# Paged sample keys: TensorE transposes replaced by VectorE 32x32 block transposes, and host matmul pieces redistributed

## Chip, cores and metric

The kernel runs on one core of one Trainium2 chip. The metric is the device time of one launch in microseconds (us), the median of several executions. Engines are named as in the profile: PE is TensorE's matmul side and PEld its weight loads, DVE is VectorE, ACT is ScalarE, POOL is GpSimd, SP is SyncE. SPq and POOLq are the queues on which SP and POOL issue DMAs.

## What is computed

Two layers of a hybrid decoder for a prompt of 1024 tokens and 8 samples of 4 new tokens each; layer 0 mixes a short convolution with differential attention. The change is in one part of layer 0: the samples' attention over a paged cache of 2048 past keys and values (16 pages of 128 rows for each sample, 4 heads of 128 numbers, all float32).

```python
past_k = cache_k[j, page_table].reshape(nb, -1, DA_HEADS, 2 * DA_DIM)
past_v = cache_v[j, page_table].reshape(nb, -1, DA_HEADS, 2 * DA_DIM)
...
s = jnp.einsum('bqhcd,bkhcd->bhcqk', q, k).astype(jnp.float32) * (DA_DIM ** -0.5)
s = jnp.where(mask, s, -jnp.inf)
p = jax.nn.softmax(s, axis=-1)
w = p[:, :, 0] - lam * p[:, :, 1]
return jnp.einsum('bhqk,bkhe->bqhe', w.astype(v.dtype), v)
```

The same layer's input projection `u @ w_in` has further columns (gates and values of the convolution) that don't depend on the samples' attention; their matmuls are spread between its steps.

## The kernel before

Every engine's program is written out by hand, in order, with semaphores. The samples' stage is `pe_samples`, `act_samples`, `dve_samples` and `sp_samples`; each is a generator of steps. `woven` runs such a generator and, after each step, as many **host pieces** as a table says: a host piece is half of a unit of the input projection (12 matmuls 128x352, fp16, line L372), and 27 units make 54 pieces. The units come in threes: three units of `gate_c` (drained from PSUM by ACT, L1513), three of the convolution's input (drained by DVE, L1574), three of `y_b` (drained by DVE, L1593, after the three convolution taps L1538 to L1545). All units of this stage use one PSUM bank, so a unit starts only when the one before it has been drained. The same weave holds for all four engines: in DVE's program a drain stands at the place at which PE's program has the second piece of that unit.

The stage works in two rounds of 4 samples. A round has a **key phase** (32 steps `q` of 2 pages), a **softmax gap**, a **value phase** (32 steps of 2 pages) and a short tail.

- Key step before: PE waits for two pages in the ring, transposes 2x4 blocks 128x128 into PSUM banks 4 and 5 (L1943), ACT and DVE copy one bank each to `kt` in SBUF (L2012, L2072), and `scores(q-1)` multiplies the turned keys of the step before with the queries in 4 matmuls (L1931), one for each head; the four write 32 partitions each of one bank. Scores of a round fill PSUM banks 0 to 3.
- Softmax gap: own keys (L1954), maxima on DVE (L2067, L2079), exponentials on ACT (L2018), and matmuls that mix the two halves (L1960 to L1967).
- Value step: 8 matmuls against 2 value pages (L1982).

Pages are 256 KB each and go into a ring of 16 (`ring`, in `hT`). `load_page` issues page `f` when `page_used` says that page `f - 16` is free; SP issues the pairs with even `f // 2`, POOL the others. `page_used` rises when PE has transposed a key page or has used a value page. SP's queue also holds the loads of projection weights (L287), each waiting until a split (L345 on DVE) has freed its buffer.

`ROUND_FILL` is the table of host pieces: before, none in the 32 key steps, 8 in the softmax gap, 15 in the value steps (one after every second), 3 in the tail.

`pool_queries` builds the block-diagonal queries `q_blk` on POOL after the key and value rows of head 3 have been stored.

Of the kernel before, what the change touches and what calls it, by code (L numbers as in the profile page):

```python
# [78 lines left out]
def build(nc, x_p, x_s, cache_k, cache_v, state_conv, state_C, state_n, state_m, page_table, norms, w_in0,  # L79
# [3 lines left out]
    with ctx:  # L83
# [1359 lines left out]
        sm_max, sm_neg = small[:, 80:85], small[:, 85:86]  # L1443
# [8 lines left out]
        wt_own = arena[0:TS, 23, 0:64]  # L1452
        comb = arena[:, 23, 64:128]
        kt = [arena[:, 24 + i, 0:SEQ].rearrange("p (h n) -> p h n", h=HEADS) for i in range(2)]
# [66 lines left out]
        def dve_proj0(dve, chain, v0, v1_):  # L1521
# [24 lines left out]
            for n in range(VISITS[v0].units[0], VISITS[v1_].units[-1] + 1):  # L1546
                v, g, x = UNITS[n].visit, UNITS[n].g, ps[:, UNITS[n].bank, :]
                h, m = (v - CXB) // 3 if v >= CXB else v // 3, v % 3
                if v >= CXB and m == 2 and g == 0:
                    if h == 0:  # L1550
                        dve.wait_ge(q_ready, 1)
# [315 lines left out]

        ROUND_FILL = ((0,) * 32 + (2, 2, 2, 2) + (1, 0) * 15 + (0, 0) + (1, 1, 1))
# [40 lines left out]
        def pe_samples(pe):  # L1909
# [1192 lines left out]
```

## Time and profile before

| | us |
|---|---|
| median of 3 runs | 2692.53 |
| lowest, highest | 2690.15, 2693.31 |
| the profiled execution's own time | 2693.54 |
| its span, first to last instruction | 2691.9 |
| PE busy, of the span | 2623.9 (97%) |
| DVE, ACT, POOL busy | 1242.1, 1026.6, 452.3 |

The profiled execution is 1.0 us above the median, and 1.6 us of its time lie outside the span. The samples' stage takes from about 315 to 574 us of the span. Busy shares are averages over stages with different limits, so the rows further down look at this stage in stretches. An "us" beside a group of several instructions is the time from the start of the first to the end of the last; the modelled duration of a single matmul is longer than the distance between two.

### The profile page before, as it was taken

To read this page: it belongs to the slowest core of one execution; us is meant where nothing else is said; L and a number is where in the kernel's file an instruction comes from. 1 tells how busy PE (TensorE), PEld (TensorE's weight loads), DVE (VectorE), ACT (ScalarE), POOL (GpSimd) and SP (SyncE) were. 2 spreads that over 40 slices of the span, in tenths; PEclk is the share of its full clock that TensorE was granted. 3 is DMA by queue.
4 is the path that set the end of the run, shared out by engine and by line. 5 is a ranking of instruction groups with operands and counts; after the bars stand their busy time and mean duration, and the time that the engine had idled before them with its cause. 6 is when DMAs were issued, how large, how long until landed. Compare 5 with 4: busy or idle time off the path is not lost.

```text
span 2691.9 us, 49459 instructions
## 1 busy us (share of the span) xinstructions
PE 2623.9 (97%) x20217; PEld 1876.5 (70%) x20217; DVE 1242.1 (46%) x2042; ACT 1026.6 (38%) x1896; POOL 452.3 (17%) x529
## 2 busy tenths in 40 slices
PE   8999899999999999999999999999999999999998
PEld 5666566656688668886566766667657886788765
DVE  5555532326744214444754434344577441154454
ACT  4455322225444214433443333324365441244333
POOL 4001023222022002311101010110101220123121
PEclk9999999999999999999999999999999999999999
DMA  7211369761211312124434242322411122011442
GB/s 250 63 40 50 98 218 346 242 230 54 75 64 32 81 53 63 48 91 146 122 88 88 40 115 50 96 67 84 151 54 67 64 60 60 32 64 48 134 129 97
DMA packets 257659, 266.14 MB, mean 99 GB/s; under 512 B 10668, under 2 KB 217810, under 8 KB 256796
## 3 DMA queue, kind: packets, MB, share of 16 engines
q1 hardware_dynamic: 231772, 166.10, 22.0%
q0 software_dynamic: 25088, 94.79, 10.0%
q8 instruction: 162, 2.65, 0.4%
q10 hardware_dynamic: 576, 2.10, 0.2%
q14 instruction: 61, 0.50, 0.1%
HBM read 227.45 MB, written 35.50 MB: 98 GB/s over the span
## 4 chain that ended last, share of the span: by engine, by line
PE 90%; DVE 5%; ACT 2%; issue 1%; DMA 0%; POOL 0%; SPq 0%; DVEq 0%; ACTq 0%; POOLq 0%
PE ps L372 49%; PE ps L1130 25%; PE ps L1943 2%; PE ps L1931 1%; PE ps L1629 1%; PE ps L1982 1%; PE ps L1708 1%; PE ps L2477 1%; PE ps L2457 1%; PE ps L2491 1%; PE ps L2513 1%; DVE arena L883 1%; PE ps L1694 1%; PE ps L2500 1%; DVE hT L887 1%
## 5 line engine op out<-in xcount | busy, mean ns | idle before, releaser
L372 PE MATMUL ps<-u,w_split 128*128 128x352 f16 (+1 forms) x4752 | 752.3, 315 | 9.8 <-DVE u L737 5.9
L372 PEld LDWEIGHTS ps<-u,w_split 128*128 128x128 f16 (+1 forms) x4752 | 462.5, 98 | 260.3 <-issue 20.8
L372 PE MATMUL ps<-arena,w_split 128*128 128x352 f16 x3663 | 560.6, 313 | 3.7 <-DVE w_split L345 1.5
L372 PEld LDWEIGHTS ps<-arena,w_split 128*128 128x128 f16 x3663 | 357.6, 98 | 200.8 <-issue 9.5
L1130 PE MATMUL ps<-hT,w_split 128*128 128x264 f16 x3456 | 400.6, 276 | 3.2 <-ACT arena L1170 3.2
L1130 PEld LDWEIGHTS ps<-hT,w_split 128*128 128x128 f16 x3456 | 337.8, 98 | 54.8 <-DVE w_split L345 2.1
L345 DVE SCALAR_TENSOR_TENSOR w_split<-w_raw,w_split 128x1024 f16<-128x1024 f32 (+2 forms) x133 | 184.5, 1388 | 296.4 <-ACT w_split L329 295.8
L1130 PE MATMUL ps<-u,w_split 128*128 128x264 f16 x2592 | 303.4, 276 | 0.0
L1130 PEld LDWEIGHTS ps<-u,w_split 128*128 128x128 f16 x2592 | 253.6, 98 | 38.3
L329 ACT ACTIVATE w_split<-w_raw 128x1024 f16<-128x1024 f32 (+2 forms) x133 | 155.5, 1171 | 135.9 <-PE ps L372 97.3
L343 DVE SCALAR_TENSOR_TENSOR w_split<-arena,w_split 128x512 f16<-128x512 f32 x126 | 85.9, 723 | 103.9 <-ACT w_split L323 103.9
L1260 POOL TENSOR_TENSOR arena<-arena 128x512 f32<-128x512 f32 x18 | 22.8, 1265 | 527.2 <-DVE w_split L343 527.2
L343 DVE SCALAR_TENSOR_TENSOR w_split<-w_raw,w_split 128x512 f16<-128x512 f32 x126 | 80.8, 686 | 62.4 <-ACT w_split L323 62.4
L372 PE MATMUL ps<-arena 128*128 128x352 f16 x657 | 102.6, 316 | 0.0
L2327 ACT ACTIVATE arena<-ps 128x352 f32<-128x352 f32 x66 | 30.5, 464 | 179.7 <-PE ps L372 179.7
L817 POOL TENSOR_TENSOR arena<-arena 128x352 f32<-128x352 f32 x53 | 71.3, 1345 | 160.5 <-ACT arena L805 160.3
L1203 DVE TENSOR_TENSOR arena<-ps,arena 128x528 f32<-128x528 f32 x36 | 25.5, 707 | 153.1 <-ACT arena L1170 153.1
L1300 ACT ACTIVATE arena<-ps 128x352 f32<-128x352 f32 x48 | 22.3, 465 | 191.3 <-PE ps L372 191.3
L372 PEld LDWEIGHTS ps<-arena 128*128 128x128 f16 x657 | 64.5, 99 | 37.0 <-issue 3.1
L1216 DVE TENSOR_TENSOR arena<-arena 128x1056 f16<-128x1056 f32 (+1 forms) x60 | 58.3, 972 | 50.4 <-ACT arena L1153 41.4
L372 PE MATMUL ps<-u,arena 128*128 128x352 f16 x504 | 77.5, 313 | 3.2 <-ACT arena L1298 2.7
L323 ACT ACTIVATE w_split<-arena 128x512 f16<-128x512 f32 x126 | 71.7, 620 | 13.7 <-PE ps L1130 10.9
(405 smaller groups left out, 2989.4 us busy)
## 6 DMA issues: line engine op xcount, KB each, us to landing
w_raw<-in_w_down SPq DMA_DIRECT2D x58, 704.0 KB, 4.7
w_raw<-in_w_in SPq DMA_DIRECT2D x56, 512.0 KB, 7.9
arena<-in_w_gu SPq DMA_DIRECT2D x18, 1024.0 KB, 5.3
w_raw<-in_w_gu SPq DMA_DIRECT2D x18, 1024.0 KB, 5.2
hT<-in_cache_k SPq DMA_DIRECT2D x64, 256.0 KB, 4.4
hT<-in_cache_k POOLq DMA_DIRECT2D x64, 256.0 KB, 4.6
hT<-in_cache_v SPq DMA_DIRECT2D x64, 256.0 KB, 5.0
hT<-in_cache_v POOLq DMA_DIRECT2D x64, 256.0 KB, 5.5
```

Of the source, the lines that this page charges most:

```text
L323: act.activation(split_of(v, 0).rearrange("p (k n) -> p k n", k=kt), raw_of(v), ACT.Copy, scale=WS).then_inc(w_hi, 1)
L329: act.activation(split_of(v, 0)[:, 0:kt * n], raw_of(v), ACT.Copy, scale=WS).then_inc(w_hi, 1)
L343: dve.scalar_tensor_tensor(lo, raw_of(v), WS, hi, ALU.mult, ALU.subtract).then_inc(w_ready, 1)
L345: dve.scalar_tensor_tensor(split_of(v, 1)[:, 0:kt * n], raw_of(v), WS, split_of(v, 0)[:, 0:kt * n], ALU.mult, ALU.subtract).then_inc(w_rea ...
L372: ins = pe.matmul(ps[0:m, bank, 0:GW], split_of(v, wp)[:, k * w + col * P:k * w + col * P + m], x[:, xp, k0 + k, cols(g)], start=(k == 0 a ...
L817: pool.tensor_tensor(sum_y, sum_y, sq_y[k % 2], ALU.add).then_inc(y_added, 1)
L883: ins = dve.scalar_tensor_tensor(h_tmp[:, k % 2, :], ybuf[:, k, cols(g)], gains[:, col:col + 1], rs[0], ALU.mult, ALU.mult)
L887: dve.tensor_tensor(h, h, h_tmp, ALU.add).then_inc(h_ready, 1)
L1130: ins = pe.matmul(ps[:, bank + s_, 0:HW], split_of(v, wp)[:, k * P:(k + 1) * P], x, start=(name in ("M1", "M2", "M5") and k == 0 and q == ...
L1216: dve.tensor_tensor(hi_lo[:, 1], x, hi_lo[:, 0], ALU.subtract).then_inc(hid_ready, 1)
L1943: ins = pe.transpose(ps[:, 4 + e, h * P:(h + 1) * P], ring[:, f % RING, h * P:(h + 1) * P], ident[:, :])
L2327: act.activation((q_of[h % 2], k1, v1, o1)[m // 2][:, m % 2, cols(g)], ps[:, UNITS[n].bank, 0:GW], ACT.Sigmoid if m >= 6 else ACT.Copy, sc ...
```

## The change

Key pages are no longer transposed by PE. DVE transposes 32x32 blocks of two ring pages at once (one instruction, 128x1024) into one row of a buffer `turned[j]`; four of them fill a buffer of 8 pages, and there are two buffers. A block transpose leaves block (i, c) in place, so the keys of partition group i and column group c lie turned within each 32x32 block. PE then scores 8 pages at once, in 64 matmuls with 32 partitions and 32 columns of weights: row group `i` uses keys 32i to 32i+31, four shifts `s_` cover the four blocks of a head, head `h` picks the column group, and row group `i` writes PSUM bank `i`. For this the queries are needed in four rotations by 32 partitions; `pool_queries` makes one and copies three by DMA, and it moves ahead of the stores of head 3. The key phases of ACT's program become empty. The maxima of a round become one reduction 128x2048. Half of the host pieces of the value steps go into the key steps: 8 in the key steps (after every fourth), 8 in the gap, 7 in the value steps, 3 in the tail. `wt_own` and `comb` move to another buffer.

```diff
-        q_blk = arena[:, 19, 0:SEQ].rearrange("p (h b n) -> p h b n", h=HEADS, b=NB)
+        Q_ROWS = (10, 12, 13, 14)
+        q_turned = [arena[:, row, 0:SEQ].rearrange("p (h b n) -> p h b n", h=HEADS, b=NB) for row in Q_ROWS]
+        q_blk = q_turned[0]
-        kt = [arena[:, 24 + i, 0:SEQ].rearrange("p (h n) -> p h n", h=HEADS) for i in range(2)]
+        turned = [rows(19 + 4 * i, 4)[:, :, 0:SEQ] for i in range(2)]
...
-            pool.wait_ge(v_ev, 3 * HEADS - 1)
+            pool.wait_ge(s_done, 16 * (HEADS - 1))
...
+            pool.wait_ge(q_copied, 2 * NB)
+            for s_ in range(1, 4):
+                cut = P - 32 * s_
+                pool.dma_start(arena[0:cut, Q_ROWS[s_], 0:SEQ], arena[32 * s_:P, Q_ROWS[0], 0:SEQ]).then_inc(q_ready, 16)
+                pool.dma_start(arena[cut:P, Q_ROWS[s_], 0:SEQ], arena[0:32 * s_, Q_ROWS[0], 0:SEQ]).then_inc(q_ready, 16)
...
-        ROUND_FILL = ((0,) * 32 + (2, 2, 2, 2) + (1, 0) * 15 + (0, 0) + (1, 1, 1))
+        ROUND_FILL = ((0, 0, 0, 1) * 8 + (2, 2, 2, 2) + (0, 1, 0, 0) * 7 + (0,) * 4 + (1, 1, 1))
...
-                def scores(q):
-
-                    n, b, j = 32 * r_ + q, 4 * r_ + q // 8, q % 8
-                    pe.wait_ge(kp_ev[0], n + 1)
-                    pe.wait_ge(kp_ev[1], n + 1)
+                def scores(n):
+
+                    b, j = 4 * r_ + n // 2, n % 2
+                    pe.wait_ge(page_used, 128 * r_ + 8 * n + 8)
                     pe.wait_ge(exps, 5 * r_)
-                    for h in range(HEADS):
-                        ins = pe.matmul(ps[32 * h:32 * h + 32, j // 2, 256 * (j % 2):256 * (j % 2) + 256],
-                                        q_blk[:, h, b, :], kt[n % 2][:, h, :], start=(b % 4 == 0 and j % 2 == 0),
-                                        stop=(b % 4 == 3), skip_group_check=True)
-                    ins.then_inc(kp_used, 1)
+                    pages = turned[j].rearrange("p a (e c) -> p a e c", e=2)
+                    for s_ in range(4):
+                        for h in range(HEADS):
+                            for i in range(4):
+                                part_, e0 = slice(32 * i, 32 * i + 32), P * h + 32 * ((i + s_) % 4)
+                                ins = pe.matmul(ps[32 * h:32 * h + 32, i, 256 * j:256 * j + 256],
+                                                q_turned[s_][part_, h, b, :], pages[part_, :, :, e0:e0 + 32],
+                                                start=(b % 4 == 0 and j == 0 and s_ == 0),
+                                                stop=(b % 4 == 3 and s_ == 3), skip_group_check=True)
+                    ins.then_inc(scored, 1)
+                for q in range(32):
+                    if q % 4 == 3:
+                        scores(q // 4)
+                    yield
...
-                    dve.wait_ge(page_used, 128 * r_ + 2 * q + 2)
-                    dve.wait_ge(kp_used, max(n - 1, 0))
-                    dve.tensor_copy(kt[n % 2][:, :, P:2 * P],
-                                    ps[:, 5, :].rearrange("p (h e) -> p h e", h=HEADS)).then_inc(kp_ev[1], 1)
+                    f = 128 * r_ + 2 * q
+                    dve.wait_ge(page_loaded[f % RING // 2], 32 * (f // RING + 1))
+                    if q >= 8:
+                        dve.wait_ge(scored, 8 * r_ + q // 4 - 1)
+                    dve.transpose(turned[q // 4 % 2][:, q % 4, :],
+                                  ring[:, f % RING:f % RING + 2, :].rearrange("p r c -> p (r c)")).then_inc(page_used, 2)
...
-                chain.link(dve.tensor_reduce(sm_max[:, 4:5], ps[:, 4, 0:TS], AX.X, ALU.max))
+                chain.mark(dve.tensor_reduce(sm_max[:, 0:1], flat(0, 4 * 512), AX.X, ALU.max))
+                chain.link(dve.tensor_reduce(sm_max[:, 1:2], ps[:, 4, 0:TS], AX.X, ALU.max))
```

PE, start of the first key phase, in the program before. L1943 are transposes, L1931 scores, and no host piece (L372) stands between:

```order
L1643 MATMUL ps<-ident,arena 128x128 x4
L1943 MATMUL ps<-ident,hT 128x128 x16
L1931 MATMUL ps<-arena 32x256 x4
L1943 MATMUL ps<-ident,hT 128x128 x8
L1931 MATMUL ps<-arena 32x256 x4
```

And now, the end of that key phase (the pair of L1938 and L372 stands there 8 times, and the last is shown):

```order
L1938 MATMUL ps<-arena 32x256 x64
L372 MATMUL ps<-u,w_split 128x352 x12
L1949 MATMUL ps<-ident,smask 128x32
L1953 MATMUL ps<-arena 32x32 x16
L372 MATMUL ps<-u,w_split 128x352 x48
```

The transposes are gone, 8 blocks of 64 small matmuls stand where 32 groups of 4 stood, and each is followed by one host piece.

DVE, end of the first round's tail and the second key phase, in the program before:

```order
L2108 SCALAR_TENSOR_TENSOR arena<-ps,gains,arena 128x16 x4
L1574 SCALAR_TENSOR_TENSOR arena<-ps,arena 128x352
L2072 COPY arena<-ps 128x4x128 x28
L2067 TENSOR_REDUCE small<-ps 128x1
L2072 COPY arena<-ps 128x4x128 x2
```

And now, from the second block's end to the fourth drain. L1575 and L1594 are drains of host units, L1539, L1542 and L1545 convolution taps:

```order
L2065 STREAM_TRANSPOSE arena<-hT 128x1024 x8
L1575 SCALAR_TENSOR_TENSOR arena<-ps,arena 128x320
L1579 SCALAR_TENSOR_TENSOR arena<-ps,arena 128x8x4
L2065 STREAM_TRANSPOSE arena<-hT 128x1024 x4
L1554 COPY conv_new<-arena 128x2
L1555 COPY conv_new<-arena 128x16
L1539 TENSOR_SCALAR arena<-arena,gains 128x1024
L1540 TENSOR_SCALAR arena<-arena,gains 128x32
L2065 STREAM_TRANSPOSE arena<-hT 128x1024 x4
L345 SCALAR_TENSOR_TENSOR w_split<-w_raw,w_split 128x1024
L1542 SCALAR_TENSOR_TENSOR arena<-arena,gains 128x1024
L1543 SCALAR_TENSOR_TENSOR arena<-arena,gains 128x32
```

Drains and taps, which stood behind the key phases, now stand between transposes, after 8, 16, 24 and 32 of them in this round, and after 24 and 32 in the first.

## Rows read from the trace of the kernel before

**Rows 1.** The page, part 4: engines' shares of the chain that ended last.
```profile
PE 90%; DVE 5%; ACT 2%; issue 1%; DMA 0%; POOL 0%; SPq 0%; DVEq 0%; ACTq 0%; POOLq 0%
```
**Rows 2.** Windows: us, busy (instructions) of PE, PEld, DVE, ACT, POOL, PE clock, DMA share, GB/s.
```profile
315.25:369.29 54.04, 53.78 (x547) 34.60 (x547) 24.61 (x36) 19.12 (x32) 17.27 (x32) 0.97 0.92 309
369.29:391.55 22.26, 20.20 (x133) 13.83 (x130) 3.83 (x11) 6.70 (x15) 0.00 (x0) 0.92 0.16 55
391.55:437.79 46.24, 46.08 (x726) 28.64 (x726) 11.80 (x21) 5.84 (x10) 15.72 (x29) 1.00 0.97 337
437.79:445.55 7.76, 6.75 (x47) 4.47 (x46) 3.10 (x12) 3.48 (x13) 1.61 (x3) 1.00 1.03 353
445.55:497.76 52.21, 51.61 (x542) 32.79 (x540) 24.66 (x37) 20.36 (x33) 17.20 (x32) 1.00 0.93 315
497.76:517.76 20.00, 18.63 (x133) 12.95 (x130) 9.48 (x23) 5.59 (x14) 0.00 (x1) 1.00 0.18 56
517.76:564.00 46.24, 46.08 (x726) 28.63 (x726) 11.27 (x20) 5.34 (x9) 13.02 (x25) 1.00 0.88 309
```
**Rows 3.** Timeline, two key steps: start, us, engine, line, what, count [idle before, releaser].
```profile
339.81 0.40 PE L1931 MATMUL ps<-arena 128*32 128x256 f32 x4
...
341.16 0.16 PEld L1931 LDWEIGHTS ps<-arena 128*32 128x32 f32 x8 [0.17 <-issue]
341.16 0.64 PE L1931 MATMUL ps<-arena 128*32 128x256 f32 x8
341.27 0.69 DVE L2072 COPY arena<-ps 128x512 f32<-128x512 f32 x1 [0.90 <-PE ps L1943]
...
341.73 1.09 PE L1943 MATMUL ps<-ident,hT 128*128 128x128 f32 x8
...
342.75 0.64 PE L1931 MATMUL ps<-arena 128*32 128x256 f32 x8
```
**Rows 4.** Timeline and one line's durations: matmuls on two row groups in layer 1.
```profile
1543.59 1.14 PE L2513 MATMUL ps<-arena,hT 32*128 32x258 f32 x8
1544.66 0.62 PE L372 MATMUL ps<-u,w_split 128*128 128x352 f16 x3
...
L2513 PE MATMUL ps<-arena,hT x128: 376/376/480, 1543.6 to 1927.2; 32*128 32x258 f32 x128
```
**Rows 5.** Timeline of DVE: single instructions of 1024 elements, one behind the other.
```profile
397.98 0.75 DVE L1538 TENSOR_SCALAR arena<-arena,gains 128x1024 f32<-128x1024 f32 x1
...
400.06 1.28 DVE L1541 SCALAR_TENSOR_TENSOR arena<-arena,gains 128x1024 f32<-128x1024 f32 x1
401.25 0.24 DVE L1542 SCALAR_TENSOR_TENSOR arena<-arena,gains 128x32 f32<-128x32 f32 x1
```
**Rows 6.** Timeline: value steps with one host piece, and the drain behind it.
```profile
395.20 1.96 PE L372 MATMUL ps<-u,w_split 128*128 128x352 f16 x12
397.10 1.06 PE L1982 MATMUL ps<-hT,arena 128*4 128x128 f32 x32
...
397.20 0.49 DVE L1574 SCALAR_TENSOR_TENSOR arena<-ps,arena 128x320 f32<-128x320 f32 x1 [5.02 <-PE ps L372]
```
**Rows 7.** Timeline: before the first key phase, and the own keys at its end.
```profile
314.15 0.75 DVE L1812 SCALAR_TENSOR_TENSOR arena<-ps,gains,arena 128x512 f16<-128x512 f32 x1 [0.40 <-ACT arena L1731]
315.25 3.67 PE L1943 MATMUL ps<-ident,hT 128*128 128x128 f32 x16 [1.86 <-issue]
...
368.46 0.90 PE L1954 MATMUL ps<-arena 128*32 128x32 f32 x32
```
**Rows 8.** Windows around the start of the first key phase (columns as in rows 2).
```profile
312.00:315.50 3.50, 1.64 (x13) 1.00 (x12) 2.50 (x3) 1.15 (x2) 0.00 (x0) 1.00 0.08 21
315.50:318.90 3.40, 3.40 (x20) 2.54 (x22) 0.69 (x1) 1.20 (x2) 0.23 (x1) 0.50 0.84 225
318.90:322.30 3.40, 3.40 (x40) 2.14 (x40) 1.53 (x3) 1.19 (x2) 0.91 (x2) 1.00 0.60 170
```
**Rows 9.** A window inside the first value phase, and DMA issues of that phase.
```profile
406.00:422.00 16.00, 16.00 (x262) 9.97 (x260) 3.24 (x5) 2.40 (x4) 5.39 (x10) 1.00 1.05 384
...
hT<-in_cache_v SPq DMA_DIRECT2D x24, 256.0 KB, 6.1
```
**Rows 10.** Timeline: two reductions 128x1024 on DVE, and the query copies on POOL.
```profile
290.59 2.35 DVE L1781 TENSOR_REDUCE small<-ps 128x1 f32<-128x1024 f32 x2
...
248.83 4.89 POOL L1863 COPY arena<-arena 64x16 f32<-64x16 f32 x16
```

More of the change, by code:

```diff
@@ L1442, in build @@
         zx, zy, zz = (small[:, 56 + 8 * i:64 + 8 * i] for i in range(3))
-        sm_max, sm_neg = small[:, 80:85], small[:, 85:86]
+        sm_max, sm_neg = small[:, 80:82], small[:, 85:86]
         sm_sum, sm_scale = small[:, 86:91], small[:, 91:92]
@@ L1550, in dve_proj0 @@
                     if h == 0:
[L1551 removed]
+                        dve.wait_ge(q_copied, 2 * NB)
                     chain.sync()
@@ L1855, in pool_queries @@
         def pool_queries(pool, chain):
-            pool.wait_ge(v_ev, 3 * HEADS - 1)
+            pool.wait_ge(s_done, 16 * (HEADS - 1))
             drained(pool, last_unit(3 * HEADS - 3))
-            chain.link(pool.memset(arena[:, 19, 0:SEQ], 0.0))
+            chain.link(pool.memset(arena[:, Q_ROWS[0], 0:SEQ], 0.0))
             for b in range(NB):
@@ L1935, in pe_samples @@
                 if r_:
                     pe.wait_ge(os_lo, 1)
-                for q in range(32):
-                    for e in range(2):
-                        f = 128 * r_ + 2 * q + e
-                        page_ready(f)
-                        pe.wait_ge(kp_ev[e], 32 * r_ + q)
-                        for h in range(HEADS):
-                            ins = pe.transpose(ps[:, 4 + e, h * P:(h + 1) * P], ring[:, f % RING, h * P:(h + 1) * P],
-                                               ident[:, :])
-                        ins.then_inc(page_used, 1)
-                    if q:
-                        scores(q - 1)
-                    yield
@@ L1949, in pe_samples @@
-                scores(31)
                 pe.matmul(ps[:, 4, 0:TS], smask[:, r_, :], ident[0:TS, 0:TS], start=True, stop=False,
@@ L2008, in act_samples @@
                 for q in range(32):
-                    n = 32 * r_ + q
-                    act.wait_ge(page_used, 128 * r_ + 2 * q + 1)
-                    act.wait_ge(kp_used, max(n - 1, 0))
-                    act.activation(kt[n % 2][:, :, 0:P], ps[:, 4, :].rearrange("p (h e) -> p h e", h=HEADS),
-                                   ACT.Copy).then_inc(kp_ev[0], 1)
                     yield
@@ L2016, in act_samples @@
                 act.wait_ge(max_ready, r_ + 1)
-                for j in range(4):
-                    act.activation(probs[:, 512 * j:512 * j + 512], ps[:, j, :], ACT.Exp, bias=sm_neg,
-                                   accum_out=sm_sum[:, j:j + 1]).then_inc(exps, 1)
+                for i in range(4):
+                    act.activation(probs[:, 0:2 * SEQ].rearrange("p (f i t) -> p i f t", i=4, t=32)[:, i],
+                                   ps[:, i, :].rearrange("p (f t) -> p f t", t=32), ACT.Exp, bias=sm_neg,
+                                   accum_out=sm_sum[:, i:i + 1]).then_inc(exps, 1)
                 act.activation(probs[:, 2 * SEQ:2 * SEQ + TS], ps[:, 4, 0:TS], ACT.Exp, bias=sm_neg,
@@ L2849, in _ @@
             for h in range(HEADS):
+                if h == HEADS - 1:
+                    pool_queries(pool, chain)
                 for ev, src, dst, n in ((v_ev, v_nat, v_p, 2), (k_ev, k_nat, k_p, 2)):
@@ L2853, in _ @@
                                    src.rearrange("p (c a e) -> p c a e", c=8, a=1)).then_inc(kv_stored, 16)
-            pool_queries(pool, chain)
             pool.wait_ge(v_ev, 3 * HEADS)
```

23 lines of the change are left out of this document (7 added, 16 removed).

## Prediction

> **What bounds the kernel now.** The page's chain comes first: nine tenths of it are PE [rows 1], so what counts is PE's time and what PE waits for. Then the windows that cut the samples' stage at its phases [rows 2]. In all four key and value phases PE is busy for all but 0.2 to 0.6 us, while ACT and DVE work less than half of a key phase; only the two softmax gaps (22.26 and 20.00 us) and the tail of round 0 (7.76) show PE waiting, 1 to 2 us each. A second column matters as much: DMAs run at 309 to 337 GB/s in the phases, and inside the value phase at 384 [rows 9]. PE bounds the stage, and a DMA limit lies close behind. Last come two key steps in the timeline [rows 3]: from one group of scores to the next 1.59 us (341.16 to 342.75), of which 0.57 are scores and 1.02 the 8 transposes.
>
> **Scores and transposes on PE.** What goes is 32 steps of 1.59 us in each round. What comes is 8 blocks of 64 matmuls. A float32 matmul is two records (4 matmuls of a step show x8), so a block has 128 records. Do small tiles overlap? In a step four records start within 0.40 us, in which each of them runs nearly its whole length, and all 8 take 0.64 [rows 3]: four column groups run at once, the second four 0.24 behind the first. L2513 does the same with two row groups: 8 records, 376 ns each, in 1.14 us, and the next group starts 1.07 after the first [rows 4]. So I take all 16 tiles of 4 row and 4 column groups to run at once, which no row shows. Then a block is 8 passes: four passes take 1.07, two take 0.57, so each further one is 0.25, and 8 are 1.07 + 4 x 0.25 = 2.1 us. Bounds: 16 passes if only 8 tiles overlap (0.57 + 14 x 0.25 = 4.1), 32 passes if only 4 do (8.1). I take 2.1, since neither the row nor the column groups cost anything for each other where they are seen. One host piece takes 1.9 us up to the next work, and the drain on DVE starts 2.0 after the piece's start and takes 0.5 [rows 6]. PE needs 2.1 + 1.9 = 4.0 us for a block.
>
> The Trainium skill, "TensorE: Matmul & The Clock Gate", Part 3, gives 10.6 times the serial speed for 16 tiles of 32x32; serial, 128 records at 0.24 us would be 31 us, and by that figure a block is 2.9 us, an estimate, 0.8 more than mine, which would add about 5 us to the whole over four drains and two tails. The same page (Part 1) says that starts of small matmuls never come closer than about 25 ns. The row with four records in 0.40 us [rows 3] speaks against it: the fourth would start 75 ns behind the first and, at 376 ns of its own [rows 4], end at 0.45. By the rule a block would be 3.2 + 0.3 = 3.5 us and the whole some 10 us above my sum, at 2690, no change; its chance is part of the second one below.
>
> **Transposes on DVE.** No row has this instruction. The nearest is a float32 instruction of 1024 elements from SBUF to SBUF: L1541, whose follower starts 1.19 us later. L1538 takes 0.75 for the same size [rows 5], and a PSUM copy 0.69 for 512 [rows 3], so 1.38 for 1024. I take 1.2, since a transpose reads and writes 1024 numbers in each partition as L1541 does, and keep 0.75 and 1.38 as ends. Four make a block: 4.8 us. So DVE, not PE (4.0), sets the pace of the key phases. The ring doesn't: 16 pages are there at the start, and at 384 GB/s 8 pages take 5.5 us, so that DVE in six blocks (28.8 us) uses what DMA can bring (16 pages, and 32 more in 22 us after the first frees).
>
> **The new wait.** A drain that stands in DVE's program behind a block of transposes waits for the host unit's second half, which PE starts only behind the scores of that same block. What is queued behind it on DVE are the next transposes, and PE waits for these in turn. So each drain costs DVE 2.1 + 2.0 + 0.5 = 4.6 us, and PE then idles 0.5 + 4.8. Round 0 has one inside (block 5) and one at the end; round 1 has three inside (blocks 1, 3, 5) and one at the end. Convolution taps moved into round 1: the first (L1539 and its small neighbours, 1.1 us by their starts) is on DVE's path, the other two with L345, 4.1 us, lie in the wait at block 3.
>
> **The clock.** Where PE had been idle 1.86 us just before 315.25 [rows 7], its clock was granted at 0.50 (1.2 GHz) from 315.5 to 318.9, and at 1.00 (2.4 GHz) next to it [rows 8]: 16 transposes took 3.67 us, 1.6 more than two groups of 8. I charge 1.7 us of PE for each idle of about 5 us. PE has 0.8 of slack in a block, so 0.9 reaches the next drain: once in round 0, three times in round 1.
>
> **Key phases.** Transposes can start when L1812 ends, at 314.90 [rows 7], where PE's start at 315.25. Round 0: 38.4 (8 x 4.8) + 4.6 (drain) + 0.9 (clock) + tail of 2.1 + 1.9 + own keys 0.8 (368.46 to 369.29) = 48.7, so it ends at 363.6 where it ended at 369.29: **-5.7**. Round 1: 38.4 + 3 x 4.6 + 0.2 (second small drain) + 1.1 (tap) + 2.7 (clock) + 4.8 (tail) = 61.0 against 52.21: **+8.8**. Eight host pieces (15 us) are done in each of them, which is why it is the value phase that gains.
>
> **Value phases.** PE's work falls from 15 to 7 pieces: 32 steps x 0.5 (two are one group of 1.06) [rows 6] + 7 x 1.9 = 29.3 us, where 15 pieces made 44.5 of the 46.24. But now DMA ends last: of 64 pages 16 are in the ring, the other 48 are 12.6 MB and take 32.8 us at 384 GB/s [rows 9]. With 3.0 until the first lands (half of the 6.1 us of a landing under full load), 1.4 for a weight tile of 0.5 MB among them and 0.5 for the last step it is 37.7 against 46.24: **-8.5 each, -17.0**.
>
> **Gaps, tail, POOL.** The drains rotate: the first gap gets the pieces that the second had, and the second nearly those of the first, so 22.26 + 20.00 stay together. The single maximum over 2048 columns takes 2.35 (two of 1024) [rows 10] where one over 512 stood behind the last scores; PE has two host pieces (3.8 us) there, which hide most of it, and I charge 0.5 a round: **+1.0** (bounds 0 and 3.4). On ACT 32 copies a round vanish, which waited for PE anyway: 0. POOL's copies (4.89 us) [rows 10] and six new DMAs stand ahead of the stores of head 3 and long before the first key phase: 0; if the stores came late, DVE's first transposes would wait for them. SP's weight loads wait for splits on DVE behind transposes; the pages queued behind them have 9 us until they are needed: 0.
>
> **Sum.** -5.7 + 8.8 - 17.0 + 1.0 = -12.9. The profiled execution took 2693.54, so 2680.6; it is 1.0 above the median of before, so I say **2680 us**.
>
> **Rivals.** (1) *Tiles overlap less.* Eight at a time: block 4.1, PE 6.0 a block, each drain 6.6. Round 0 becomes 4.8 + 48 + 5.3 + 0.8 = 59 (before 54.4 from 314.90), round 1 four pairs of 4.8 + 6.0 + 4.1 + 2.5 and 0.3 = 70: +4.6 + 18 - 17 + 1 gives 2700. Four at a time: 8.1, so 10.0 a block and 86 in either round: +31 + 34 - 17 + 1 gives 2742. For it: no row has more than four at once, and four row groups would write four banks of the same partitions together. Against it: rows 3 and 4. It decides from a block of 3.9 us upwards, where round 1 has eaten the value phases' gain. This is the case that ends slower. (2) *Slower transposes.* At 1.38 us, +11.5, so 2691: no change. At twice my value 77 us more, 2757; nothing in the rows speaks for that. (3) *DMA doesn't hold 384 GB/s.* At the value phases' mean of 337, 48 pages take 37.3 and a phase 42.4, so only -3.8 each: 2689. For it: the DMA share is 0.97 already in that phase; against it: the 16 us at 384. (4) *DVE is faster.* At 0.75 a block of transposes is 3.0 and PE's 4.0 sets the pace: 14 us less in round 0, 4 in round 1, with the value phases 2658.
>
> **Chances.** My forecast with its own spread (2672 to 2687) 0.45; rivals 2 (mild) and 3, and the forecast's upper edge, 2687 to 2698, 0.19; eight tiles or a mixture, 2698 to 2708, 0.13; four tiles or very slow transposes 0.12; rival 4 and anything below 2672, 0.11. Range 2662 to 2708: it leaves out 0.12 above and some 0.05 below. A measurement tells 0.2% (5.4 us): faster 0.56, same 0.18, slower 0.26.
>
> **What will show it.** Transposes of 1.2 us, one behind the other but for one long wait on PE in the first key phase and three in the second, each ended by L372. Groups of 128 records of 32x32 in about 2.1 us. Stretches of granted clock 0.50 behind these waits. Value phases of about 38 us in which PE waits for DMA of value pages, with 380 GB/s. Key phases of about 49 and 61 us. I am wrong if a scoring block takes over 3 us, if DVE doesn't wait for L372, or if PE still ends the value phases without waiting for pages.

## Result and profile after

| | before | after |
|---|---|---|
| median, us | 2691.69 (4 runs) | 2703.06 (4 runs) |
| lowest, highest | 2690.15, 2693.31 | 2700.26, 2708.56 |
| profiled execution, its span | 2693.54, 2691.9 | 2700.58, 2699.0 |

The change makes the kernel slower: ratio 1.005, 95% interval 1.0038 to 1.0062, so 10 to 17 us. I had said 2680, 13 us faster. The profiled execution of after is 7.0 us above that of before, at the low end of its runs.

The page, part 4 (the chain that ended last), answers [rows 1]. PE holds 74% of it where it held 90%:

```profile
PE 74%; DVE 4%; ACT 2%; issue 1%; DMA 1%; SPq 1%; POOL 0%; DVEq 0%; ACTq 0%
```

Windows of after, answering [rows 2] (us, busy of PE, PEld, DVE, ACT, POOL, PE clock, DMA share, GB/s): key phase, gap, value phase, tail, and the second round's key phase, gap and value phase.

```profile
313.50:372.52 59.02, 43.59 (x1154) 26.25 (x1155) 39.20 (x37) 3.16 (x4) 17.28 (x32) 0.88 0.87 305
372.52:395.66 23.14, 20.31 (x133) 13.56 (x131) 11.67 (x24) 5.59 (x14) 0.00 (x0) 0.93 0.08 24
395.66:436.91 41.25, 33.34 (x629) 21.04 (x629) 3.53 (x5) 3.78 (x6) 15.87 (x30) 0.92 0.97 350
436.91:445.76 8.85, 7.67 (x44) 4.19 (x40) 3.05 (x12) 3.44 (x12) 1.33 (x3) 0.81 1.05 374
445.76:512.98 67.22, 45.66 (x1154) 27.90 (x1155) 44.26 (x49) 3.05 (x5) 17.37 (x32) 0.82 0.78 263
512.98:533.58 20.60, 18.54 (x133) 12.90 (x131) 6.97 (x13) 7.61 (x18) 0.00 (x0) 1.00 0.11 31
533.58:575.45 41.87, 32.75 (x630) 21.18 (x629) 7.78 (x15) 1.55 (x2) 13.12 (x24) 0.96 0.92 326
```

In both key phases PE, busy for all of them before, now idles 15 and 22 us, at a mean clock of 0.88 and 0.82. Against before, with the first key phase counted from 314.90 as in the prediction: key phases +4.6 and +15.0, value phases -5.0 and -4.4, gaps +0.9 and +0.6, tail +1.1, and the stage begins 1.4 earlier. That is +11.4 at the end of the second value phase (575.45 for 564.00). Behind the stage 4.3 us of it come back; there before's clock is lower in places (0.97 for 1.00 from 575 to 700 us), which the change doesn't touch.

Timeline of DVE in after, from the sixth block of the first key phase on (start, us, engine, line, what, count, idle before and its releaser):

```profile
341.33 4.62 DVE L2065 STREAM_TRANSPOSE arena<-hT 128x1024 f32<-128x1024 f32 x4 [1.70 <-PE ps L1938]
345.88 1.18 DVE L345 SCALAR_TENSOR_TENSOR w_split<-w_raw,w_split 128x1024 f16<-128x1024 f32 x1
...
354.68 0.53 DVE L1575 SCALAR_TENSOR_TENSOR arena<-ps,arena 128x352 f32<-128x352 f32 x1 [7.47 <-PE ps L372]
355.12 9.12 DVE L2065 STREAM_TRANSPOSE arena<-hT 128x1024 f32<-128x1024 f32 x8
371.46 0.53 DVE L1575 SCALAR_TENSOR_TENSOR arena<-ps,arena 128x352 f32<-128x352 f32 x1 [7.23 <-PE ps L372]
```

Transposes are as forecast, 4.62 us a block. From their end at 345.95 to the next at 355.12 there are 9.2 us, where I had 5.5 with the clock. PE at the same time:

```profile
336.35 0.69 PE L1938 MATMUL ps<-arena 32*32 32x256 f32 x26
338.88 2.31 PE L1938 MATMUL ps<-arena 32*32 32x256 f32 x102 [1.83 <-issue]
...
348.54 2.76 PE L1938 MATMUL ps<-arena 32*32 32x256 f32 x128
351.23 0.32 PE L372 MATMUL ps<-u,w_split 128*128 128x352 f16 x1
352.82 1.81 PE L372 MATMUL ps<-u,w_split 128*128 128x352 f16 x11 [1.27 <-issue]
359.79 4.53 PE L1938 MATMUL ps<-arena 32*32 32x256 f32 x128 [5.15 <-DVE arena L2065]
```

A scoring block takes 2.76 us at full clock and 4.53 behind this idle of 5 us (4.08 to 4.52 behind those of the second key phase). And there is something that I hadn't thought of: inside a block, or a host piece, PE stands for 0.4 to 1.8 us with nothing to wait for ("issue"; such an idle is called a stall below). A window of that idle and block, and the next, with the clock in the last column but two:

```profile
358.80:365.60 6.80, 5.81 (x133) 3.42 (x134) 5.44 (x5) 0.00 (x0) 2.69 (x5) 0.50 0.89 312
365.60:369.40 3.80, 3.80 (x136) 2.40 (x134) 0.00 (x0) 0.00 (x0) 1.08 (x2) 1.00 1.04 395
```

The second key phase on DVE has the three inner waits and the one at the end:

```profile
462.87 0.49 DVE L1575 SCALAR_TENSOR_TENSOR arena<-ps,arena 128x320 f32<-128x320 f32 x1 [7.99 <-PE ps L372]
...
478.94 0.53 DVE L1594 SCALAR_TENSOR_TENSOR arena<-ps,arena 128x352 f32<-128x352 f32 x1 [1.17 <-PE ps L372]
...
495.63 0.52 DVE L1594 SCALAR_TENSOR_TENSOR arena<-ps,arena 128x352 f32<-128x352 f32 x1 [6.73 <-PE ps L372]
...
511.92 0.52 DVE L1594 SCALAR_TENSOR_TENSOR arena<-ps,arena 128x352 f32<-128x352 f32 x1 [6.33 <-PE ps L372]
```

### The profile page after: what moved, and what is told of

Its sections match the earlier page's. It is cut to its first block, busy times and chain, and to the rows that moved or that the text cites. A ratio compares the mean times of both kernels' runs of the same rounds, so it can differ in the third digit from the quotient of the medians.

```text
span 2699.0 us, 51203 instructions
## 1 busy us (share of the span) xinstructions
PE 2576.1 (95%) x21241; PEld 1844.4 (68%) x21241; DVE 1268.8 (47%) x2036; ACT 988.3 (37%) x1832; POOL 455.9 (17%) x535
## 4 chain that ended last, share of the span: by engine, by line
PE 74%; DVE 4%; ACT 2%; issue 1%; DMA 1%; SPq 1%; POOL 0%; DVEq 0%; ACTq 0%
PE ps L372 41%; PE ps L1130 25%; PE ps L2468 1%; PE ps L2448 1%; PE ps L2482 1%; PE ps L2504 1%; DVE arena L883 1%; PE ps L2491 1%; DVE hT L887 1%; DVE arena L897 1%; DMA hT<-in_cache_v 1%; PE ps L2532 1%; PE ps L1938 1%; PE ps L2483 1%; DVE arena L2065 0%
## 5 line engine op out<-in xcount | busy, mean ns | idle before, releaser
L372 PE MATMUL ps<-u,w_split 128*128 128x352 f16 (+1 forms) x4752 | 754.2, 315 | 12.9 <-DVE u L737 5.9
L372 PEld LDWEIGHTS ps<-u,w_split 128*128 128x128 f16 (+1 forms) x4752 | 462.6, 99 | 268.6 <-issue 27.2
L372 PE MATMUL ps<-arena,w_split 128*128 128x352 f16 x3663 | 559.0, 313 | 3.7 <-DVE w_split L345 1.5
L372 PEld LDWEIGHTS ps<-arena,w_split 128*128 128x128 f16 x3663 | 357.0, 98 | 199.7 <-issue 9.4
L345 DVE SCALAR_TENSOR_TENSOR w_split<-w_raw,w_split 128x1024 f16<-128x1024 f32 (+2 forms) x133 | 184.4, 1387 | 285.1 <-ACT w_split L329 284.6
L372 PE MATMUL ps<-arena 128*128 128x352 f16 x657 | 101.0, 313 | 0.0
L2318 ACT ACTIVATE arena<-ps 128x352 f32<-128x352 f32 x66 | 30.5, 464 | 179.7 <-PE ps L372 179.7
L1938 PE MATMUL ps<-arena 32*32 32x256 f32 x2048 | 56.5, 466 | 37.6 <-DVE arena L2065 32.4
L372 PEld LDWEIGHTS ps<-arena 128*128 128x128 f16 x657 | 64.0, 98 | 36.2 <-issue 3.1
L372 PE MATMUL ps<-u,arena 128*128 128x352 f16 x504 | 79.0, 316 | 3.2 <-ACT arena L1298 2.7
```

Of the source, the lines that this page charges most:

```text
L345: dve.scalar_tensor_tensor(split_of(v, 1)[:, 0:kt * n], raw_of(v), WS, split_of(v, 0)[:, 0:kt * n], ALU.mult, ALU.subtract).then_inc(w_rea ...
L372: ins = pe.matmul(ps[0:m, bank, 0:GW], split_of(v, wp)[:, k * w + col * P:k * w + col * P + m], x[:, xp, k0 + k, cols(g)], start=(k == 0 a ...
L1938: ins = pe.matmul(ps[32 * h:32 * h + 32, i, 256 * j:256 * j + 256], q_turned[s_][part_, h, b, :], pages[part_, :, :, e0:e0 + 32], start=(b ...
L2318: act.activation((q_of[h % 2], k1, v1, o1)[m // 2][:, m % 2, cols(g)], ps[:, UNITS[n].bank, 0:GW], ACT.Sigmoid if m >= 6 else ACT.Copy, sc ...
```

## Experiments

The theory behind them: the places of host pieces in the key phases, with drains that wait, cost what the transposes and the value phases give. The rival: the scoring blocks themselves, by their length, the half clock and the issue stalls, are too slow wherever the pieces stand. Kernel before had a median of 2689.2 to 2689.7 us beside them (2691.69 beside after); each ratio is against the runs beside it. "Key phases" are from the first transpose to the end of the own keys, in us. Line numbers move by one to three between kernels. The three "unloaded" kernels have one run each, so their totals can't be set against a scatter of 6 to 16 us in the others; what is read from them are the lengths of phases in their profiles.

| kernel | median | ratio to before (95%) | key phases |
|---|---|---|---|
| after | 2703.06 | 1.0038 to 1.0062 | 59.0, 67.2 |
| fill_back | 2688.03 | 0.9978 to 1.0000 | 49.9, 48.8 |
| before_new_fill | 2709.09 | 1.0056 to 1.0089 | |
| drains_later | 2696.59 | 1.0018 to 1.0038 | 59.0, 59.7 |
| splits_aligned | 2686.79 | 0.9977 to 0.9996 | 54.8, 55.2 |
| kept_warm | 2701.01 | 1.0026 to 1.0057 | 58.2, 64.4 |
| half_scores | 2682.46 | 0.9959 to 0.9986 | 50.3, 57.5 |
| pieces_first | 2683.05 | 0.9961 to 0.9982 | 56.2, 54.8 |
| six_in_keys | 2687.99 | 0.9979 to 1.0000 | 50.9, 54.4 |
| four_in_keys | 2690.25 | 0.9993 to 1.0010 | 51.3, 57.3 |
| keys_unloaded | 2692.02, one run | | 52.4, 67.2 |
| back_unloaded | 2667.52, one run | | 41.1, 40.1 |
| values_unloaded | 2687.82, one run | | 60.3, 68.2 |

**fill_back: only the table of pieces undone.**

```diff
-ROUND_FILL = ((0, 0, 0, 1) * 8 + (2, 2, 2, 2) + (0, 1, 0, 0) * 7 + (0,) * 4 + (1, 1, 1))
+ROUND_FILL = ((0,) * 32 + (2, 2, 2, 2) + (1, 0) * 15 + (0, 0) + (1, 1, 1))
```

> The changed kernel with the old table of host pieces: none in the key phases, 15 in each value phase. Theory (the host pieces and their drains in the key phases are what costs): DVE sets the pace, 8 blocks of 4.62 us, then one scoring block of 2.7 and the own keys, 0.8: 40.5 us a key phase, 44 with some issue stalls; value phases back at 46.2. Against the changed kernel's 59.0 + 67.2 + 41.25 + 41.9 that is 174 to 181 for 209, so 2672 to 2680, below the kernel before. Rival (the scoring blocks themselves are too slow, wherever the pieces stand): PE, idle for 2 us in each block, stays at the half clock, a block takes 4.5 us and issue stalls of 1 us come on top, so PE sets 5.5 a block: 48 us a key phase, 2689, no better than before.

2688.0: the rival's number. Going back to the old table wins 15 us (2703 to 2688), the whole loss; the transposes on DVE by themselves gain between 0 and 0.2%. PE in its first key phase:

```profile
332.48 4.51 PE L1938 MATMUL ps<-arena 32*32 32x256 f32 x127 [0.60 <-issue]
338.79 4.07 PE L1938 MATMUL ps<-arena 32*32 32x256 f32 x128 [1.80 <-issue]
344.83 4.07 PE L1938 MATMUL ps<-arena 32*32 32x256 f32 x127 [1.97 <-issue]
```

Each of these rows begins in the middle of a block and runs into the next. From one to the next it takes 4.7 to 6.0 us where DVE needs 4.6. Stalls and half clock come together here, but a stall doesn't always lower the clock: in after, five stalls of up to 1.83 us left it at 1.00 from 322 to 358 us.

The rival's account fits the first key phase only. In the second, PE waits for DVE (15.5 us in seven places), and DVE for key pages. DVE in the first key phase:

```profile
328.20 5.84 DVE L2065 STREAM_TRANSPOSE arena<-hT 128x1024 f32<-128x1024 f32 x5 [1.82 <-issue]
334.99 2.37 DVE L2065 STREAM_TRANSPOSE arena<-hT 128x1024 f32<-128x1024 f32 x2 [0.94 <-DMA hT<-in_cache_k]
```

The first of these waits is put down to issue, but the trace has the landing of the page that it reads 0.08 us before it starts, and so it is, within 0.12 us, for every transpose that waited for "issue" in these kernels. Late pages cost DVE 3.7 and 4.1 us in fill_back's key phases, and 1.7 and 0 in after's.

**before_new_fill: the table alone, in the kernel before** (the same two lines the other way round).

> The kernel before with the new table of host pieces: 8 in each key phase, 7 in each value phase. Theory (the value phases become DMA-bound, so that moving pieces out of them doesn't pay even): PE bounds the key phases, +8 x 1.9 = +15.2 each; the value phases end by DMA at about 41.5 for 46.24, -4.7 each; +21 in sum, 2713. Rival (moving is neutral, since PE has the same work): 2692. If the waits of drains behind key steps cost extra here too, more than 2713.

2709.1, 20 above before. The first key phase goes from 54.0 to 66.7 us (315.96 to 382.67), +12.7 for 8 pieces (in a profiled execution 5 us above the median), the first value phase from 46.24 to 44.0 (402.67 to 446.65), since DMA ends it. So moving pieces out of value phases is a loss by itself while PE bounds the key phases.

**drains_later: the places on DVE one block later.**

```diff
+ROUND_LATE = ((0,) * 4 + (0, 0, 0, 1) * 6 + (0, 0, 0, 2) + (2, 2, 2, 2) + (0, 1, 0, 0) * 7 + (0,) * 4 + (1, 1, 1))
-woven(dve_samples(dve, chain), dve_proj0(dve, chain, CXB + 3, WO0 - 1), SAMPLE_FILL)
+woven(dve_samples(dve, chain), dve_proj0(dve, chain, CXB + 3, WO0 - 1), (1, 1, 0) + ROUND_LATE * 2)
```

> The changed kernel with the pieces' places on DVE one block (4 steps) later than on PE in the key phases; the last two fall together at the end of the phase. A drain then finds its unit done. Theory (the waits of drains cost 4 x about 8 us): PE sets the pace with 2.75 + 1.9 = 4.65 a block; first key phase 4.6 + 37.2 + 0.8 + issue stalls of 3 to 5 = 46 to 48 for 59.0, the second 48 to 52 for 67.2 (its taps, 4.1 us of DVE, now lie open): -26 or so, 2675 to 2681. Rival (issue stalls and the half clock set PE's time, and the waits only hide them): first phase unchanged at 57 to 59, second about 58: 2690 to 2695.

Neither: 2696.6, and the first key phase is no shorter. The inner drain waits 1.68 for 7.47 us, but a new wait has come, on DVE and SP's queue (timeline):

```profile
351.29 1.18 DVE L345 SCALAR_TENSOR_TENSOR w_split<-w_raw,w_split 128x1024 f16<-128x1024 f32 x1
352.55 0.39 SPq L287 DMA_DIRECT2D w_raw<-in_w_in  x1
353.70 4.30 SPq L1883 DMA_DIRECT2D hT<-in_cache_k  x4
...
360.67 4.62 DVE L2066 STREAM_TRANSPOSE arena<-hT 128x1024 f32<-128x1024 f32 x4 [5.85 <-DMA hT<-in_cache_k]
```

The split (L345) is later too; the weight load (L287) waits for it on SP's queue, and four key pages stand behind that load.

**splits_aligned: SP's places later as well.**

```diff
-woven(sp_samples(sp), sp_proj0(sp, CXB + 3, WO0 - 1), SAMPLE_FILL)
+woven(sp_samples(sp), sp_proj0(sp, CXB + 3, WO0 - 1), (1, 1, 0) + ROUND_LATE * 2)
```

> As drains_later, and SP's places for the weight loads are one block later too, so that a weight load doesn't wait on SP's queue, with key pages behind it, for a split that now comes one block later on DVE. Theory (the 5.85 and 5.14 us for which DVE waited for key pages in drains_later come from that): both waits go, -9 to -11, so 2686 to 2689 beside drains_later's 2696.6. Rival (the DMAs were full and the pages late anyway): no change, 2695 to 2697.

Held: both waits for pages are gone, -9.8 us. With the inner drains no longer waited for, the kernel is 16 us below after; DVE's remaining long wait of the first phase, 6.76, is the drain behind its last block. One of its 10 runs took 10509 us; I have no cause for it. Without it the median is 2686.22.

**kept_warm: 28 transposes of the identity ahead of the blocks that follow a long wait.**

```diff
+                    if n == 6 or (r_ and n % 2 == 0):
+                        for _ in range(28):
+                            pe.transpose(ps[:, 5, 0:P], ident[:, :], ident[:, :])
```

> The changed kernel with 28 transposes of the identity into an unused PSUM bank (about 3.7 us) ahead of the scoring blocks that follow a long idle: block 6 of the first key phase, blocks 0, 2, 4 and 6 of the second. They fill the idle of 5.2 us and add no wait. Theory (the half clock behind an idle makes a block 4.5 for 2.75 us and passes this on to the next drain): 1.8 to 3 us less at each of 3 to 4 drains, -7, so 2696 for 2703. Rival (the clock's loss lies in slack and costs nothing): 2703. If the added instructions stall as well, up to 2 us more.

2701.0: not to be told from after. Three of the five blocks ran in 2.75 behind idles of 2.1 to 2.2 us, and two in 4.1 at lower clock behind 2.1 and 2.3:

```profile
458.13 3.22 PE L1933 MATMUL ps<-ident 128*128 128x128 f32 x28
463.69 4.08 PE L1941 MATMUL ps<-arena 32*32 32x256 f32 x128 [2.34 <-DVE arena L2068]
```

The key phases are 0.8 and 2.8 us shorter in the profile. So the clock, though plain in the rows, is worth some 4 us there by this one profile, where the medians differ by 2, less than their scatter. The remedy was only half tried: it kept the full clock three times of five.

**half_scores: two of four shifts.** Half of the scoring is left out.

```diff
-                    for s_ in range(4):
+                    for s_ in range(2):
-                                                stop=(b % 4 == 3 and s_ == 3), skip_group_check=True)
+                                                stop=(b % 4 == 3 and s_ == 1), skip_group_check=True)
```

> The changed kernel with two of the four shifts, so half of the scoring matmuls is left out (64 records a block) and the scores are not the attention's. It prices a scoring block. Theory (a block's length counts once for each of the 4 inner drain waits and the 2 tails, 1.35 us at full clock and 2.2 at half, and its issue stalls go to half): -8 to -13, so 2690 to 2695. Rival (PE's time in the blocks is hidden behind DVE's transposes, and only the waits for the host pieces count): -3 or less, 2700.

2682.5: -20.6, more than the theory said. A block is 1.50 us, at half clock 2.38, and PE shows no stall by issue at all. So the 20.6 are the price of half the matmuls and of all stalls together. What is left on DVE inside the first key phase, ahead of its drain, are late pages, 4.2 us.

**keys_unloaded: one row of each key page.**

```diff
-            eng.dma_start(ring[:, f % RING, :], cache[0, ds(page, 1), :, :, :].rearrange("a t h e -> (a t) (h e)")
+            n = 1 if f // 64 % 2 == 0 else P
+            eng.dma_start(ring[0:n, f % RING, :], cache[0, ds(page, 1), 0:n, :, :].rearrange("a t h e -> (a t) (h e)")
```

> The changed kernel with one row of 128 loaded from each key page (the other rows of the ring are what was there), so the scores are of other numbers and nearly no DMA traffic runs in the key phases. Theory (PE's instructions are fetched by DMA, and page loads hold them up): the idle time put down to issue inside the scoring blocks, 5.4 us in the first key phase and 1.6 in the second, goes to below 1; first key phase about 54, second 65. Rival (128 records in 2.7 us are more than PE's queue can feed at any time): the issue stalls stay as they are, and the key phases too.

Held for the first phase, 52.4; with the same instructions PE's block is 2.75 or 2.76 every time but behind waits, and one starts every 4.58 us (timeline of PE):

```profile
334.97 2.76 PE L1939 MATMUL ps<-arena 32*32 32x256 f32 x128
337.66 1.96 PE L372 MATMUL ps<-u,w_split 128*128 128x352 f16 x12
339.55 2.75 PE L1939 MATMUL ps<-arena 32*32 32x256 f32 x128
```

The second stays at 67.2: its waits and half clocks are there without any page traffic. PE's waits in after from 313 to 515 us (engine, line, waited for: us in total, times, longest):

```profile
PE ps L1938 <- DVE arena L2065: 32.4, 6, 6.3
PE ps L1981 <- DMA hT<-in_cache_v: 7.8, 5, 2.8
PE ps L1938 <- issue: 5.2, 5, 1.8
```

The same in pieces_first (further down):

```profile
PE ps L1939 <- issue: 9.5, 8, 2.5
PE ps L1939 <- DVE arena L2066: 6.7, 4, 2.5
PE ps L372 <- issue: 3.9, 2, 2.1
```

And one DMA queue in pieces_first from 313 to 510 us (packets, MB, share of 16 engines):

```profile
q8 instruction: 25, 0.41, 0.8%
```

Before and half_scores have 17 packets there, keys_unloaded 25 without a stall. The stalls need both, 64 small matmuls a block and full DMAs. The kept traces show that PE then waits for its instructions: they have the start and length of each packet of that queue (16 KB each). Nine of these kernels have stalls of over 0.35 us between the first scores and 515 us, 66 in all, and every one ends 1.2 to 1.6 us after such a packet has ended, a stretch that makes up about a twentieth of the time. The stall that ends at 338.88 in after, for one, has its packet from 336.23 to 337.29. The packets aren't longer beside the page loads (1.02 us in the mean in after, 1.12 in keys_unloaded); what holds them up before they start isn't in the traces.

**pieces_first: a block's piece ahead of its scores, on PE alone.**

```diff
+ROUND_PE = ((1, 0, 0, 0) * 8 + (2, 2, 2, 2) + (0, 1, 0, 0) * 7 + (0,) * 4 + (1, 1, 1))
-woven(pe_samples(pe), pe_halves(pe, range(3 * CXB + 9, 3 * WO0), u), SAMPLE_FILL)
+woven(pe_samples(pe), pe_halves(pe, range(3 * CXB + 9, 3 * WO0), u), (1, 1, 0) + ROUND_PE * 2)
```

> The changed kernel, but PE runs a key block's host piece before the block's scores instead of behind them; the places on DVE, ACT and SP stay. The piece then runs while DVE transposes that block, and its drain behind the transposes finds it done. Theory (waits of drains, and the tail of 1.9 us, are what makes the key phases long): 4.6 until the first scores, then 7 x 4.65 + 2.75 + 0.8 = 41, plus 5 us of issue stalls in the first phase, plus 5 us for taps in the second: 46 and 49 for 59.0 and 67.2, -31, so about 2672 to 2680, below the kernel before. Rival (with no waits left the page loads end the phase, 48 pages at 384 GB/s after 3 us: 36 us at least, and more issue stalls come with them): 52 each, 2686 to 2690.

2683.05, 20 below after and 0.2 to 0.4% faster than before: the best whole kernel here. PE's waits for DVE fell from 32.4 to 6.7 us; what I missed is that the stalls grew from 6.5 to 13.5 us (with 1.9 in the own keys). By the rows above they would be 15.3, but 1.83 of L372's 3.9 is the idle before the first piece, which the kernel before has too (1.86 [rows 7]) and where after waits for DVE. PE in the first key phase, with the piece in the idle ahead of the first scores, and a stall:

```profile
314.16 3.12 PE L372 MATMUL ps<-u,w_split 128*128 128x352 f16 x12 [1.83 <-issue]
318.42 4.08 PE L1939 MATMUL ps<-arena 32*32 32x256 f32 x128 [1.15 <-DVE arena L2066]
...
361.47 2.07 PE L1939 MATMUL ps<-arena 32*32 32x256 f32 x91
366.00 2.15 PE L1939 MATMUL ps<-arena 32*32 32x256 f32 x37 [2.46 <-issue]
```

In after a stall could be hidden in part in a wait for DVE; here PE waits little, so I take it that most of a stall counts. No run prices that.

**four_in_keys and six_in_keys: pieces_first with 4 and 6 pieces in the key phases.** The key and value parts of PE's table in pieces_first, four_in_keys and six_in_keys, in this order; the other engines' table changes with it.

```diff
-(1, 0, 0, 0) * 8 ... (0, 1, 0, 0) * 7 + (0,) * 4
+(1, 0, 0, 0, 0, 0, 0, 0) * 4 ... (1, 0, 0) * 10 + (1, 0)
+(1, 0, 0, 0) * 6 + (0,) * 8 ... (0, 1, 0) * 9 + (0,) * 5
```

> As pieces_first, with 4 host pieces in each key phase (ahead of the scores of every second block) and 11 in each value phase for 8 and 7. Theory (in pieces_first PE, with 8 us of issue stalls, sets the pace of the key phases, while PE has slack in the value phases, which DMA ends at 41 us): PE needs 8 x 2.75 + 4 x 1.9 + 8 = 38, so DVE sets the pace with 4.62 a block, 4.6 + 37 + 0.8 = 43 to 45 for about 54 in each key phase; value phases stay at 41 to 42, since 32 x 0.5 + 11 x 1.9 = 37. That is -15 to -20 on pieces_first's 2683: 2664 to 2668. Rival (PE's idle of 2 us in every second block brings the half clock, as in fill_back, and stalls stay): 48 each, 2674 to 2678. Or the value phases are bound by PE as well: 2680.

> As four_in_keys, with 6 pieces in each key phase (ahead of the scores of the first six blocks) and 9 in the value phases. Theory of DVE's pace with stalls of PE: PE needs 22 + 11.4 + 8 = 41, so 46 to 48 each, 2668 to 2673, between the two. Rival (the half clock decides; PE is kept busier here): better than four_in_keys.

A miss: 2690.3 and 2688.0, both above pieces_first; the two differ by less than their scatter. Stalls don't shrink (four_in_keys: 13.1 us in scores), pages come late (3.7 and 6.5 us of DVE's time in four_in_keys, 4.2 and 1.8 in six_in_keys), a block without a piece leaves PE idle, and in four_in_keys SP's queue again holds key pages behind a weight load that waits for the split of 481.96 (timeline of DVE and PE):

```profile
491.83 4.62 DVE L2066 STREAM_TRANSPOSE arena<-hT 128x1024 f32<-128x1024 f32 x4 [5.29 <-DMA hT<-in_cache_k]
...
496.51 4.52 PE L1939 MATMUL ps<-arena 32*32 32x256 f32 x128 [10.41 <-DVE arena L2066]
```

How the loss splits between these isn't settled. The half clock isn't needed for it: six_in_keys ran its first key phase at a granted clock of 1.00 throughout, and it still took 50.9 us, with 7.8 of stalls.

**back_unloaded: fill_back and keys_unloaded together.**

> fill_back (no host piece in the key phases) with one row of 128 loaded from each key page, as in keys_unloaded. In fill_back a key phase took 50 us where DVE's transposes alone are 37, PE worked at the half clock in most blocks, and blocks were held up by issue. Theory (stalls of PE's instruction fetch under page traffic make the difference; a block at half clock, 4.5 us, still fits beside 4.6 us of transposes): without traffic DVE sets the pace, 4.6 + 7 x 4.6 + a block of 2.75 to 4.5 + 0.8 to 1.3 = 41 to 44. Rival (the half clock itself makes the blocks too long, with DVE waiting for scores): 48 or more, DVE waiting for PE in most blocks.

Held: 41.1 and 40.1 us for the key phases where fill_back took 49.9 and 48.8.

```profile
331.83 2.75 PE L1939 MATMUL ps<-arena 32*32 32x256 f32 x128 [1.75 <-DVE arena L2066]
336.33 2.75 PE L1939 MATMUL ps<-arena 32*32 32x256 f32 x128 [1.75 <-DVE arena L2066]
```

DVE sets the pace, 4.51 us a block, and an idle of 1.75 us before each block leaves the clock at 1.00 (a window of the same stretch):

```profile
330.00:338.00 8.00, 4.50 (x225) 3.16 (x228) 8.00 (x8) 0.00 (x0) 3.41 (x7) 1.00 0.03 6
```

So page traffic is what takes fill_back's gain, and it does so in two ways that this run takes away together: late pages on DVE, 3.7 and 4.1 us of the 8.8 and 8.7 between the two kernels, and PE's stalls with the half clock beside them.

**values_unloaded: one row of each value page**, the same edit with the phases exchanged.

> The changed kernel with one row of 128 loaded from each value page, so the values summed are others and the value phases have nearly no DMA traffic. Theory (DMA ends the value phases, as I took it in the sum): each falls from 41.3 and 41.9 to PE's own 29.5 us, 2679. Rival (PE's order, its clock or the page waits of single steps set it): 35 or more, 2690.

The value phases fall from 41.3 and 41.9 to 33.8 and 33.6, not to 29.5: some waits for DMA remain near their ends (1.36 us the longest), and PE is busy for 30.6 and 30.5. Nearer to the theory: the loads of value pages cost 7.4 and 8.3 us in them.

## Why the prediction was wrong, step by step

- **Scores.** The 16 tiles do overlap. I took 2.1 us; it is 2.75, inside my bounds. The estimate of 2.9 us, worked out from the speed-up of 10.6 that the Trainium skill states ("TensorE: Matmul & The Clock Gate", Part 3), was nearer. Its rule of 25 ns between starts (Part 1) would have made 3.5 if it is taken by records; 128 records in 2.76 us, the last of about 0.4, start 19 ns apart in the mean, and the first 16 of the block at 348.54 start 6 or 7 ns apart, so this measurement speaks against it. Counted by matmuls, of two records each, the mean is 37 ns, which doesn't.
- **Transposes.** 4.62 a block for 4.8: right, and rivals 2 and 4 fell. That DVE sets the pace came true throughout only without page traffic (back_unloaded). "The ring doesn't" was right in the mean and wrong at places: 8 pages take 5.5 us to load and 4.62 to transpose, and DVE waited 1.7 us for late pages in after's first key phase.
- **The new wait.** Right in kind and number of places, wrong in size. I took 4.6 us each. Measured from transposes to transposes: 9.2 in round 0 and 8.7, 5.6 (taps inside) and 7.6 in round 1, and 7.8 to 8.3 at the ends for 4.8. The step that failed is "PE has 0.8 of slack in a block". Even at full clock a block and a piece take 4.58 us (keys_unloaded) where four transposes take 4.6, so there is no slack, and a delay is never worked off. Behind a wait the block is 4.1 to 4.5 and the piece 2.0 to 2.6, together 5.9 to 7.0 us against 4.6 of transposes, so PE comes 1.3 to 2.4 us late to the block whose drain DVE waits for (0.3 where a tap holds DVE up as well), and then needs 2.75 + 1.9 + 0.5. In round 0 the lateness at the inner drain comes from the first block at half clock (3.92) and from stalls: 6.9 us from transposes to transposes without stalls (keys_unloaded), 9.2 with them.
- **The clock.** The stretches at 0.50 are there, up to 6.8 us long, where the row that I went by had 3.4. kept_warm's profile gives some 4 us for them in the key phases, with two of its five blocks still slow.
- **Key phases.** Forecast -5.7 and +8.8, measured +4.6 and +15.0. Round 0 is 10.3 over: 2.8 by DVE's waits for scores before the drain (stalls, and the first block's half clock) and 1.7 by late pages, 3.7 in the drain's wait (1.3 of it a stall), 3.5 at the end, less 1.4 for faster transposes. Round 1 is 6.2 over: 5.1 in the three waits, 3.0 at the end, less 1.8 for faster transposes. keys_unloaded parts the causes: without page traffic its phases of 52.4 and 67.2 are still 3.7 and 6.2 above my sum, by the slack that wasn't there and the clock; the other 6.6 of round 0 go with the traffic. The stalls weren't in the sum at all, a term put at nothing without a reason, and no rival had them.
- **Value phases.** Forecast -8.5 each, measured -5.0 and -4.4. DMA does end them, and rival 3 (384 GB/s don't hold) is not why. Windows of 4 us from its start, the first two and the fourth:

```profile
395.66:399.66 4.00, 4.00 (x89) 2.93 (x92) 2.19 (x3) 1.44 (x2) 1.08 (x2) 1.00 0.46 124
399.66:403.66 4.00, 4.00 (x88) 2.51 (x80) 0.00 (x0) 0.46 (x1) 1.70 (x4) 1.00 0.97 317
...
407.66:411.66 4.00, 1.08 (x36) 0.85 (x40) 0.00 (x0) 0.00 (x0) 1.61 (x3) 0.79 1.04 388
```

  From 404 us on it is 356 to 392. The terms that were too small are the bytes and the start. The whole phase moved 350 GB/s x 41.25 us = 14.4 MB, where I had 13.1: a second weight tile and pages of the next round are among them. 14.4 MB at 385 and 3.4 us lost at the start are 40.9.
- **Gaps, tail, start.** +1.0 forecast and +1.5 measured for the gaps; the tail's +1.1 is one piece at half clock (3.40 us); the start 1.4 early.
- **The chances.** 0.26 stood on slower, most of it on tiles that don't overlap. The 2703 lies in the band that I gave to eight tiles at a time or a mixture, but the tiles do overlap; that my range holds it is luck. The sign came from another quarter: -12.9 was the difference of terms that each leaned on a slack (PE's 0.8 us, DMA's last MB), and both were gone.

## What to carry to other kernels

When two engines hand blocks back and forth, put a drain only where its producer ran a block earlier: moving PE's piece ahead of the scores was worth 20 us here, more than the change itself. Whatever is moved on one engine's program takes its splits and loads with it; look who waits behind these on SP's queue. And count instructions, not only busy time: 64 small matmuls a block beside full DMAs brought stalls of 0.4 to 2.9 us, which were gone with half of the matmuls and gone without the page loads.

## What the hardware showed that I had not expected

- Stalls of PE by issue under page traffic: 6.5 us from 313 to 515 in after, 13.5 in pieces_first, none in keys_unloaded and half_scores; each ended 1.2 to 1.6 us behind a packet of the instruction queue.
- Some of these kernels scatter more than before: six_in_keys ran from 2678.0 to 2694.4 in 12 runs, the kernel before from 2684.9 to 2693.9 in 23 beside it, and pieces_first only from 2680.8 to 2686.4 in 8. I have no cause for it.
- An idle of 1.75 us before every block kept the full clock (back_unloaded), while idles of 2.1 to 2.3 us after 28 transposes of 128x128 kept it three times and lost it twice (kept_warm). What decides isn't shown.
